# Output tiles of the attention summed in parts between its last heads, decay sums over 128 rows, key rotation spread over four tiles

## The chip, the cores and the metric

One core of a Trainium2 chip runs the kernel alone. The metric is the device time of one execution, in microseconds (us). The engines are TensorE (PE, with its weight loads as PEld), VectorE (DVE), ScalarE (ACT), GpSimd (POOL) and SyncE (SP), which issues the weight transfers. Each engine works through its own list of instructions in order and waits on semaphores for the others.

## The reference, cut to what matters

The input is x, 512 tokens by 1024. Two blocks follow one another: a block of a Mamba-2 layer and an attention layer with latent keys and values, and a block of feed-forward, a second mixer and feed-forward. All matrices are fp32. What the change touches is this:

```python
# Mamba-2 scan, one chunk: decays between tokens from running sums cum of dt * A
seg = cum[:, :, None] - cum[:, None, :]
L = jnp.exp(jnp.where(causal, seg, -jnp.inf))
...
# latent keys and values: the rotated part of the key is shared by all 16 heads
ckv, k_rope = jnp.split(hn @ w_dkv, [KV_LORA], axis=-1)
ckv = rms_norm(ckv, g_ckv)
k_rope = apply_rope(k_rope, cos, sin)
...
# attention of 16 heads, causal; then gate, output projection, residual
cq, gate = jnp.split(h @ w_in, [Q_LORA], axis=-1)
q = (rms_norm(cq, g_q) @ w_uq).reshape(Bsz, S, MLA_HEADS, QK_NOPE + QK_ROPE)
p = jax.nn.softmax(jnp.where(mask, s, -jnp.inf), axis=-1).astype(v.dtype)
o = o.reshape(Bsz, S, MLA_HEADS * V_HEAD) * jax.nn.silu(gate)
return o @ w_out
```

## The kernel before, in words

Activations lie with features on the partitions: a matrix of 1024 features by 512 tokens is eight tiles of 128 x 512. A weight is read in units of at most 128 x 1024 fp32, in the order of `unit_order()`; there are four buffers `raw` for what the transfers bring, and three pairs `wr`/`wl`. Each fp32 value is split into a high part that TensorE's fp32r format holds and the rest. A product is then three matmuls of 128 x 128 by 128 x 512 (`three`, L675 to L678): high by high, high by low, low by high. The high part of a unit is copied by ACT (`hi()`, L1030), the low part is `raw - wr` on DVE (`lo()`, L1324). Both run two units ahead of TensorE (`AHEAD`): a unit's `hi()` waits until the unit three before it is used up (`s_unit`), its `lo()` until `hi()` is done (`s_hi`), and TensorE takes the unit when `s_lo` has counted it. For the eight units `qa`/`qb` of the attention's queries and keys alone, `lo()` makes the high copy on DVE (L1320), ACT does nothing, and POOL makes the low part (L1996). A unit of a 1024-row matrix feeds one output tile: eight steps over its input tiles, 24 matmuls.

The order of work on every engine is written out by hand; there is no planner. `Banks` records in which of the eight PSUM banks a result goes and which semaphore must be reached before the bank may be written again.

The Mamba-2 layer (`first_mixer`). For each pair of heads q = 0 to 15, `decays(q)` (L747) makes two matmuls that spread the row of a head over all partitions: the stationary operand is a column of `pick`, a constant that adds a high and a low row, the moving one is `CH`, 64 rows by 512 (high rows 0 to 31, low rows 32 to 63). ACT turns the result into exponentials `LL` (L1079 to L1088), DVE multiplies them (L1561), and TensorE sums them (L761). Between these stand the tiles of the input projection, one unit each.

The latents (`latents`). Four units `kv_down` give two latent tiles and the key's rotated part in banks 0, 1 and 2. Then eleven output tiles of `mla_in` follow in the order `MLA_ORDER`: four gates, three query latents, four gates. In step i DVE calls `lo()` for the unit two ahead, does side work, and then scales tile i out of PSUM (`SG`, L1659, or the latent, L1651). ACT calls `hi()` and then applies SiLU to the scaled tile (L1169), in this order: so `hi()` of step i+1 stands behind the SiLU of step i, and that behind DVE's scaling of step i. DVE's side work of step 0 is: row scale (L1373), the two latent tiles with their low parts (L1611, L1613), one fold of squares (L1334), and the whole rotation of the key with its copies for the four key buffers `KH` (L1618 to L1634, 12 instructions). The sum of squares `ck` is read on TensorE in step 2 (L686), turned into an inverse root by POOL (L1981 to L1990), and spread in step 4 (L696).

The attention (`attention`). Step h, 0 to 17, does on TensorE: transposes of head h-2 (`turn_most`, L873), scores of head h (L868), the last transposes of head h-2 (`turn_rest`), a projection piece for later heads (`project(h)`, steps 0 to 12 only, L676 to L678 from `CQ` or `CK`), and at odd h the values of a pair (`values`, L896). DVE finds row maxima (L1711) and scales (L1719), ACT makes the exponentials (L1206), scales (L1197) and copies transposed pieces out of PSUM (`PT`, L1182), which frees bank 5 for `turn_rest`. The output of pair j becomes input tile j of the output projection: DVE gates it (`OT`, L1726), ACT makes its high part (L1043), DVE the low part (L1340). After the last step come the eight output tiles `mla_out`, each 24 matmuls; after each tile DVE adds the residual (L1491), ACT squares it twice (L1035, L1039), then makes the next unit's high part. Before TensorE's first projection stands a wait for all eight value tiles in SBUF (`s_vt`, 8). The first pieces use banks 0, 1, 0, of which bank 0 was the last value tile's.

## Time and profile before

| | |
|---|---|
| three timed runs | 1887.38, 1888.96, 1889.33 us; median 1888.96 |
| the profiled execution | 1890.32 us, of which its span is 1888.3 |
| TensorE matmul busy | 1827.4 us, 97% of the span, 8276 matmuls |
| DVE busy | 1035.7 us, 55% |
| ACT busy | 729.0 us, 39% |
| POOL busy | 53.8 us, 3% |
| mean granted clock of TensorE | 0.989 of full |
| transfers | 163.82 MB, queue q1 27.5% of 16 engines |

The span is the time from the first to the last instruction in the profile; the rest of the execution's time lies around it. A row of the timeline gives start and length in us, engine, line, operation, result and inputs, the shape and a count of merged instructions. In brackets stand the engine's idle time before it and what ended it. A matmul's length covers more than its turn, since matmuls overlap: the time that one costs is the distance of two starts. "Granted clock" is TensorE's clock that the throttle let through; 1.00 is 2.4 GHz and 0.5 is 1.2 GHz.

### The profile page before, as it was taken

The numbers are of one execution on the slowest core, as the hardware profiler recorded it, in microseconds if no ns is written. First come the engines' busy times: TensorE is split into PE (matmuls) and PEld (weight loads), VectorE is DVE, ScalarE is ACT, GpSimd is POOL, SyncE is SP. The second block draws the span as 40 slices with busy tenths as digits, with TensorE's granted clock in tenths as the row PEclk, the third lists the DMA queues.
The fourth block names the chain that finished last, engine by engine and source line by source line (L and its number), as shares of the span: only waits on it lengthen the run. The fifth ranks groups of instructions, "written<-read, shape, count | busy, mean of one in ns | idle before, by whom it ended". The sixth has DMA issues, their size and how long they took to land.

```text
span 1888.3 us, 20951 instructions
## 1 busy us (share of the span) xinstructions
PE 1827.4 (97%) x8276; PEld 1460.4 (77%) x8276; DVE 1035.7 (55%) x1484; ACT 729.0 (39%) x1197; POOL 53.8 (3%) x122
## 2 busy tenths in 40 slices
PE   6899999998999899999999999999999999999997
PEld 5677776877866578888888878888888888888886
DVE  6888876666477556444433336555443554444333
ACT  4577776333356643333222243222222333323221
POOL 2000101100120000000000000000000000000000
PEclk9999999999999999999999999999999999999998
DMA  4121212222211023333333422333333333332331
GB/s 149 66 68 67 79 56 78 92 89 70 90 59 34 12 89 91 106 94 100 95 93 94 132 78 80 99 101 92 98 101 100 90 96 94 101 98 90 103 93 53
DMA packets 47041, 163.82 MB, mean 87 GB/s; under 512 B 5216, under 2 KB 5472, under 8 KB 46944
## 3 DMA queue, kind: packets, MB, share of 16 engines
q1 hardware_dynamic: 46656, 162.29, 27.5%
q8 instruction: 66, 1.08, 0.2%
q14 instruction: 31, 0.25, 0.0%
q10 hardware_dynamic: 288, 0.20, 0.0%
HBM read 160.37 MB, written 2.10 MB: 86 GB/s over the span
## 4 chain that ended last, share of the span: by engine, by line
PE 86%; DVE 7%; ACT 4%; issue 2%; POOL 0%; DMA 0%; SPq 0%; DVEq 0%; ACTq 0%; POOLq 0%
PE pb L676 26%; PE pb L678 25%; PE pb L677 25%; PE pb L761 2%; PE pb L868 1%; DVE wl L1324 1%; PE pb L873 1%; PE pb L970 1%; PE pb L972 1%; PE pb L971 1%; DVE XL L1342 1%; ACT wr L1030 1%; PE pb L896 1%; PE pb L686 1%; DVE LL L1561 1%
## 5 line engine op out<-in xcount | busy, mean ns | idle before, releaser
L676 PE MATMUL pb<-XR,wr 128*128 128x512 f32 x1592 | 633.5, 398 | 24.0 <-DVE wl L1324 12.7
L677 PE MATMUL pb<-XL,wr 128*128 128x512 f32 x1592 | 623.5, 392 | 0.0
L678 PE MATMUL pb<-XR,wl 128*128 128x512 f32 x1592 | 623.1, 391 | 0.0
L1324 DVE TENSOR_TENSOR wl<-raw,wr 128x1024 fp32r<-128x1024 f32 (+1 forms) x298 | 359.5, 1206 | 409.9 <-ACT wr L1030 409.0
L1030 ACT ACTIVATE wr<-raw 128x1024 fp32r<-128x1024 f32 (+1 forms) x298 | 309.5, 1038 | 269.3 <-PE pb L678 243.4
L676 PEld LDWEIGHTS pb<-XR,wr 128*128 128x128 f32 x1592 | 301.5, 189 | 97.5 <-issue 27.0
L678 PEld LDWEIGHTS pb<-XR,wl 128*128 128x128 f32 x1592 | 301.0, 189 | 63.8
L677 PEld LDWEIGHTS pb<-XL,wr 128*128 128x128 f32 x1592 | 301.4, 189 | 60.2 <-issue 0.3
L1039 ACT ACTIVATE SQ<-H 128x512 f32<-128x512 f32 x42 | 26.4, 632 | 129.8 <-DVE H L1488 61.2
L676 PE MATMUL pb<-ffn1HR,wr 128*128 128x512 f32 x176 | 68.5, 389 | 0.0
L677 PE MATMUL pb<-ffn1HL,wr 128*128 128x512 f32 x176 | 68.5, 389 | 0.0
L678 PE MATMUL pb<-ffn1HR,wl 128*128 128x512 f32 x176 | 68.5, 389 | 0.0
L676 PE MATMUL pb<-ffn2HR,wr 128*128 128x512 f32 x176 | 68.5, 389 | 0.0
L677 PE MATMUL pb<-ffn2HL,wr 128*128 128x512 f32 x176 | 68.5, 389 | 0.0
L678 PE MATMUL pb<-ffn2HR,wl 128*128 128x512 f32 x176 | 68.5, 389 | 0.0
L1477 DVE SCALAR_TENSOR_TENSOR CV<-U,vec,CV 128x512 f32<-128x512 f32 x72 | 54.3, 754 | 2.6
L676 PE MATMUL pb<-YR,wr 128*128 128x512 f32 x128 | 50.1, 391 | 1.5 <-DVE wl L1324 1.5
L1238 ACT ACTIVATE ffn2HR<-ffn2UP 128x512 fp32r<-128x512 f32 x22 | 13.9, 633 | 97.1 <-DVE ffn2UP L1792 97.1
L678 PE MATMUL pb<-YR,wl 128*128 128x512 f32 x128 | 49.8, 389 | 0.0
L677 PE MATMUL pb<-YL,wr 128*128 128x512 f32 x128 | 49.8, 389 | 0.0
L1238 ACT ACTIVATE ffn1HR<-ffn1UP 128x512 fp32r<-128x512 f32 x22 | 13.9, 633 | 90.4 <-DVE ffn1UP L1792 90.4
L1561 DVE TENSOR_TENSOR LL<-LL,CB 128x1024 f32<-128x1024 f32 (+1 forms) x64 | 48.4, 818 | 0.0
(315 smaller groups left out, 2229.0 us busy)
## 6 DMA issues: line engine op xcount, KB each, us to landing
raw<-in_ffn_in SPq DMA_DIRECT2D x88, 512.0 KB, 3.5
raw<-in_mix_in SPq DMA_DIRECT2D x48, 512.0 KB, 3.5
raw<-in_ssm_in SPq DMA_DIRECT2D x41, 512.0 KB, 3.3
raw<-in_ffn_out SPq DMA_DIRECT2D x32, 512.0 KB, 3.5
raw<-in_ffn_out SPq DMA_DIRECT2D x16, 384.0 KB, 3.1
raw<-in_mla_in SPq DMA_DIRECT2D x11, 512.0 KB, 3.2
raw<-in_ssm_out_a SPq DMA_DIRECT2D x8, 512.0 KB, 3.2
raw<-in_ssm_out_b SPq DMA_DIRECT2D x8, 512.0 KB, 3.3
```

Source lines behind the costliest of these rows:

```text
L676: e.matmul(o, r, xr, start=first, stop=False)
L677: e.matmul(o, r, xl, start=False, stop=False)
L678: return e.matmul(o, l, xr, start=False, stop=last)
L686: m = e.matmul(o[:, at + i:at + i + 1], accs[key][:, 128 * i:128 * i + 128], ones[:, 0:1], start=True, stop=True)
L761: m = e.matmul(y[64 * p:64 * p + 64, 128 * k:S], XD[:, k, j, 64 * p:64 * p + 64], LL[q % 2][:, p, 512 * k:512 * k + S - 128 * k], start=k ...
L868: e.matmul(o[:, at:at + n], q[:, 128 * i:128 * i + 128], kh[:, 0:n], start=True, stop=False)
L1030: e.activation(wr[j % NS][:, 0:width(j)], raw[j % NR][:, 0:width(j)], ACT.Copy).then_inc(s_hi, 1)
L1039: e.activation(SQ[i][:, :], src, ACT.Square, scale=gain).then_inc(s_sq, 1)
L1238: e.activation(HRS[f][:, t, :], UPS[f][t % 2][:, :], ACT.Copy).then_inc(s_hhi, 1)
L1324: e.tensor_tensor(wl[j % NS][:, 0:width(j)], raw[j % NR][:, 0:width(j)], wr[j % NS][:, 0:width(j)].bitcast(F32), ALU.subtract).then_inc(s_ ...
L1477: e.scalar_tensor_tensor(out=cv, in0=u[:, k:k + S], scalar=col("conv_w", 4 * ch + k), in1=cv, op0=ALU.mult, op1=ALU.add).then_inc(then(s_c ...
L1561: m = e.tensor_tensor(x, x, CB[g % 2][:, OFF[k]:OFF[k] + d].unsqueeze(1).to_broadcast([128, 2, d]), ALU.mult)
```

## The change

Five edits:

1. `pick` and `CH` get 128 rows, rows 64 to 127 zero. The 32 matmuls of `decays` are over 128 rows. POOL clears `CH` with one more memset at the start.
2. In the latents, DVE's fold of `ck` and the rotation are spread: fold, first product and two copies in step 1, six instructions in step 2, the last two sums and the three copies to `KH` in step 3. One wait between them is dropped. ACT makes the high copies of the latents ahead of their squares.
3. TensorE's wait for `s_vt` moves from ahead of the projections into `values`. The first three projection pieces use banks 7, 1, 0.
4. `OUT_PARTS`: the matmuls of output tiles 0 and 1, and of tile 2 at the end, are issued step by step between the last heads. A pair (n, t) is three matmuls, tile n over input tile t. 14 pairs stand in steps 13 to 17, ten behind them. The accumulation of tiles 0 and 1 stays open in banks 0 and 1 meanwhile.
5. The high parts of `mla_out` 0 and 1 are made by DVE (in its `lo()` of steps 9 and 10, ahead of the low part), no longer by ACT. High and low part of `mla_out` 2 are made in step 13, no longer after the last head.

```diff
--- before.py
+++ after.py
@@ -105,6 +105,13 @@
     for g in (1, 2, 3):
         out += [[("q", g, 0), ("k", g, 0)], [("q", g, 1)], [("q", g, 2)], [("k", g, 1)]]
     return out + [[], [], []]
+
+OUT_PARTS = {13: [(0, 0), (0, 1)], 14: [(0, 2), (0, 3), (0, 4)], 15: [(0, 5), (1, 0), (1, 1)],
+             16: [(1, 2), (1, 3), (1, 4), (1, 5)], 17: [(0, 6), (1, 6)],
+             18: [(2, 0), (2, 1), (2, 2), (2, 3), (0, 7), (1, 7), (2, 4), (2, 5), (2, 6), (2, 7)]}
 
 
 def ssm_steps():
@@ -321,13 +328,13 @@
-    pick = low("pick", [64, 32], F32R, ph2)
+    pick = low("pick", [128, 32], F32R, ph2)
-    CH = low("CH", [64, S], F32R, ph2)
+    CH = low("CH", [128, S], F32R, ph2)
@@ -440,6 +447,9 @@
 
     seq = unit_order()
     unit = {name: i for i, name in enumerate(seq)}
+
+    POOL_LO = range(unit["qa", 0], unit["qb", 3] + 1)
+    DVE_HI = range(unit["qa", 0], unit["mla_out", 1] + 1)
     steps, last_gates, tail = ssm_steps()
     convs = [x[1] for x in steps if x[0] == "conv"]
     conv_no = {n: i for i, n in enumerate(convs)}
@@ -538,9 +548,13 @@
         for i in range(4):
             bk.place(("v", hf, i), ring.next(), (s_v, 3 * hf + i + 1) if i < 3 else whole("ukv_v", hf),
                      (s_vt, 4 * hf + i + 1))
-    ring = Ring([0, 1])
-
     pieces = head_steps()
+
+    def place_parts(h):
+        for n, t in OUT_PARTS.get(h, ()):
+            if t == 0:
+                bk.place(("mo", n), (0, 1, 2)[n], whole("mla_out", n), (s_res, 8 + n + 1))
+
 
     def place_project(h):
         for kind, g, i in pieces[h + 1]:
@@ -550,8 +564,12 @@
             else:
                 bk.place(("k", g, i), ring.next(), whole(("qa", "qb")[i], g), (s_kh, 4 * g + 2 * i + 2))
 
+    ring = Ring([7, 1, 0])
     place_project(-1)
+    ring = Ring([0, 1])
     for h in range(18):
+        if h == 17:
+            place_parts(h)
         if h >= 2:
             bk.place(("pt", h - 2, 0), 5, (s_turn, 3 * h - 5), (s_pt, 3 * h - 5))
             bk.place(("pt", h - 2, 1), 6, (s_turn, 3 * h - 4), (s_pt, 3 * h - 4))
@@ -563,10 +581,13 @@
             bk.place(("pt", h - 2, 2), 5, (s_turn, 3 * h - 3), (s_pt, 3 * h - 3))
         if h < 16:
             place_project(h)
+        if h < 17:
+            place_parts(h)
         if h >= 3 and h % 2 == 1:
             bk.place(("o", h // 2 - 1), 7, (s_val, h // 2), (s_ot, h // 2))
-    ring = Ring([0, 1, 2, 4, 5, 6])
-    for n in range(8):
+    place_parts(18)
+    ring = Ring([4, 5, 6, 0, 1, 2])
+    for n in range(3, 8):
         bk.place(("mo", n), ring.next(), whole("mla_out", n), (s_res, 8 + n + 1))
 
     def place_ffn(f):
@@ -748,7 +769,7 @@
-                e.matmul(o[:, :], pick[:, h:h + 1].to_broadcast([64, 128]), CH[:, :], start=True,
+                e.matmul(o[:, :], pick[:, h:h + 1].to_broadcast([128, 128]), CH[:, :], start=True,
@@ -888,6 +909,7 @@
         def values(j):
 
             o = opened(("o", j))
+            w.wait_ge(s_vt, 8)
             for k, piece in ((0, 1), (1, 2), (3, 2), (2, 3)):
                 n = S - 128 * k
                 for p in range(2):
@@ -897,11 +919,26 @@
                                  PT[p][:, TOFF[k]:TOFF[k] + n], start=k == 0, stop=k == 2)
             m.then_inc(s_val, 1)
 
+        out_weights = {}
+
+        def out_parts(h):
+            for n, t in OUT_PARTS.get(h, ()):
+                if t == 0:
+                    opened(("mo", n))
+                    out_weights[n] = take("mla_out", n)
+                o, (r, l) = PB[bk.bank["mo", n]], out_weights[n]
+                w.wait_ge(s_xlo, tile_x(3, t))
+                c = slice(128 * t, 128 * t + 128)
+                m = three(o[:, :], r[:, c], l[:, c], XR[:, t, :], XL[:, t, :], t == 0, t == KT - 1)
+                if t == KT - 1:
+                    m.then_inc(s_unit, 1)
+
         def attention():
             w.wait_ge(s_cqlo, 3)
-            w.wait_ge(s_vt, 8)
             project(-1)
             for h in range(18):
+                if h == 17:
+                    out_parts(h)
                 if h >= 2:
                     turn_most(h - 2)
                 if h < 16:
@@ -910,9 +947,12 @@
                     turn_rest(h - 2)
                 if h < 16:
                     project(h)
+                if h < 17:
+                    out_parts(h)
                 if h >= 3 and h % 2 == 1:
                     values(h // 2 - 1)
-            for n in range(8):
+            out_parts(18)
+            for n in range(3, 8):
                 o = opened(("mo", n))
                 r, l = take("mla_out", n)
                 for t in range(KT):
@@ -1021,7 +1061,7 @@ (ACT, hi)
-            if j >= len(seq) or seq[j][0] in ("qa", "qb"):
+            if j >= len(seq) or j in DVE_HI:
@@ -1157,13 +1197,13 @@
                     for t in range(2):
                         w.wait_ge(s_craw, t + 1)
                         w.wait_ge(s_rot, 1)
+                        e.activation(CK[:, 0, t, :], craw[t], ACT.Copy, scale=col("kv_g_latent", t)).then_inc(s_ckhi, 1)
                         square(("ck", t), craw[t])
-                        e.activation(CK[:, 0, t, :], craw[t], ACT.Copy, scale=col("kv_g_latent", t)).then_inc(s_ckhi, 1)
                 if n < 3:
                     w.wait_ge(s_craw, 3 + n)
+                    e.activation(CQ[:, 0, n, :], craw[2 + n], ACT.Copy, scale=col("g_q", n)).then_inc(s_cqhi, 1)
                     w.wait_ge(s_sums, sums_no["ck"])
                     square(("cq", n), craw[2 + n])
-                    e.activation(CQ[:, 0, n, :], craw[2 + n], ACT.Copy, scale=col("g_q", n)).then_inc(s_cqhi, 1)
                 else:
                     w.wait_ge(s_sg, n - 2)
                     e.activation(SG[:, n - 3, :], SG[:, n - 3, :], ACT.Silu).then_inc(s_sgs, 1)
@@ -1205,7 +1245,7 @@
                         n = 128 * (i + 1)
                         e.activation(pp[:, POFF[i]:POFF[i] + n], PB[b][:, at:at + n], ACT.Exp, bias=sm[:, 1, i:i + 1],
                                      scale=SCALE, accum_out=sm[:, 2, i:i + 1]).then_inc(s_exp, 1)
-                if h < 11 and h % 4 in (1, 2):
+                if h < 11 and h % 4 in (1, 2) or h == 13:
                     hi()
                 if h >= 2 and h % 2 == 1:
                     j = h // 2 - 1
@@ -1213,7 +1253,8 @@
                     x_hi(j, OT[:, :], None)
             w.wait_ge(s_gain, 1)
             for n in range(8):
-                hi()
+                if n:
+                    hi()
                 if n == 7:
                     for t in range(7):
                         w.wait_ge(s_mlo, t + 1)
@@ -1313,11 +1354,12 @@
             n_lo[0] += 1
             if j >= len(seq):
                 return
-            if seq[j][0] in ("qa", "qb"):
+            if j in DVE_HI:
                 w.wait_ge(s_hi, j)
                 w.wait_ge(s_raw[j % NR], 16 * (j // NR + 1))
                 w.wait_ge(s_unit, j - NS + 1)
                 e.tensor_copy(wr[j % NS][:, 0:width(j)], raw[j % NR][:, 0:width(j)]).then_inc(s_hi, 1)
+            if j in POOL_LO:
                 return
             w.wait_ge(s_lo, j)
             w.wait_ge(s_hi, j + 1)
@@ -1613,19 +1655,21 @@
                         e.scalar_tensor_tensor(out=CK[:, 1, t, :], in0=craw[t], scalar=col("kv_g_latent", t),
                                                in1=CK[:, 0, t, :].bitcast(F32), op0=ALU.mult,
                                                op1=ALU.subtract).then_inc(s_cklo, 1)
+                if i == 1:
                     fold("ck", 1)
                     w.wait_ge(s_rot, 1)
-                    e.tensor_tensor(TQ[64:128, :], TB[64:128, :], RS[64:128, :], ALU.mult).then_inc(c.up(), 1)
-                    w.wait_ge(c.h, c.n)
+                    e.tensor_tensor(TQ[64:128, :], TB[64:128, :], RS[64:128, :], ALU.mult)
                     e.tensor_copy(TA[64:96, :], TB[96:128, :])
                     e.tensor_copy(TA[96:128, :], TB[64:96, :]).then_inc(c.up(), 1)
+                if i == 2:
                     w.wait_ge(c.h, c.n)
-                    e.tensor_tensor(TS[64:128, :], TA[64:128, :], RS[64:128, :], ALU.mult)
+                    e.tensor_tensor(TS[64:128, :], TA[64:128, :], RS[64:128, :], ALU.mult).then_inc(c.up(), 1)
                     e.tensor_tensor(KH[0][64:96, :], PB[2][64:96, :], TQ[64:96, :], ALU.mult)
-                    e.tensor_tensor(OT[64:96, :], PB[2][96:128, :], TQ[96:128, :], ALU.mult).then_inc(c.up(), 1)
+                    e.tensor_tensor(OT[64:96, :], PB[2][96:128, :], TQ[96:128, :], ALU.mult)
                     w.wait_ge(c.h, c.n)
                     e.tensor_tensor(KH[0][96:128, :], PB[2][64:96, :], TS[64:96, :], ALU.mult)
                     e.tensor_tensor(OT[96:128, :], PB[2][96:128, :], TS[96:128, :], ALU.mult).then_inc(s_kr, 1)
+                if i == 3:
                     w.wait_ge(s_kr, 1)
                     e.tensor_tensor(KH[0][64:96, :], KH[0][64:96, :], OT[64:96, :], ALU.add)
                     e.tensor_tensor(KH[0][96:128, :], KH[0][96:128, :], OT[96:128, :], ALU.subtract).then_inc(c.up(), 1)
@@ -1719,6 +1763,8 @@
                     e.tensor_scalar(p, p, sm[:, 3, 3:4], None, ALU.mult).then_inc(s_pwd, 1)
                 if h < 16:
                     project(h)
+                if h == 13:
+                    lo()
                 if h >= 2 and h % 2 == 1:
                     j = h // 2 - 1
                     w.wait_ge(*bk.full["o", j])
@@ -1729,7 +1775,8 @@
             e.tensor_tensor(gain2[:, :], vec[:, a:a + KT], vec[:, b:b + KT], ALU.mult).then_inc(s_gain, 1)
             w.wait_ge(s_gain, 1)
             for n in range(8):
-                lo()
+                if n:
+                    lo()
                 if n == 7:
                     for t in range(7):
                         x_lo(4, t, H[:, t, :], gain2[:, t:t + 1])
@@ -1932,7 +1979,8 @@
         e.memset(pick[:, :].bitcast(F32), 0.0).then_inc(s_const, 1)
-        w.wait_ge(s_const, 7)
+        e.memset(CH[:, :].bitcast(F32), 0.0).then_inc(s_const, 1)
+        w.wait_ge(s_const, 8)
...
```

## Rows read from the trace of the kernel before

**Rows 1.** Waits of PE: line, who was waited for, us in total, times, longest

```profile
PE pb L676 <- DVE wl L1324: 14.3, 5, 6.0
...
PE pb L873 <- ACT PT L1182: 4.3, 3, 2.0
...
PE pb L873 <- ACT PP L1197: 3.4, 2, 1.7
```

**Rows 2.** Windows: stretch, length, busy time by engine, granted clock, DMA share, GB/s

```profile
84.00:234.00 150.00, 150.00 (x707) 106.52 (x703) 125.89 (x176) 107.70 (x208) 5.21 (x13) 0.99 0.20 67
234.00:294.20 60.20, 57.87 (x278) 41.75 (x277) 40.89 (x58) 45.18 (x90) 0.00 (x0) 1.00 0.18 62
...
594.00:655.20 61.20, 52.13 (x295) 32.76 (x294) 35.79 (x77) 43.17 (x122) 0.00 (x0) 0.97 0.06 18
```

**Rows 3.** Timeline of PE in the latents

```profile
467.04 0.77 PE L676 MATMUL pb<-XR,wr 128*128 128x512 f32 x1 [6.05 <-DVE wl L1324]
...
472.28 0.40 PE L676 MATMUL pb<-XR,wr 128*128 128x512 f32 x1
```

**Rows 4.** Timeline of DVE in the latents

```profile
454.81 0.69 DVE L1334 TENSOR_TENSOR ACC<-ACC,SQ 128x512 f32<-128x512 f32 x1
...
462.13 1.10 DVE L1634 COPY KH<-KH 64x512 f32<-64x512 f32 x3
463.26 0.69 DVE L1659 TENSOR_TENSOR SG<-pb,RS 128x512 f32<-128x512 f32 x1
465.66 1.23 DVE L1324 TENSOR_TENSOR wl<-raw,wr 128x1024 fp32r<-128x1024 f32 x1 [1.71 <-ACT wr L1030]
```

**Rows 5.** Timeline of ACT in the latents

```profile
450.20 0.63 ACT L1035 ACTIVATE ACC<-PP 128x512 f32<-128x512 f32 x1 [5.05 <-DVE PP L1611]
...
463.99 0.63 ACT L1169 ACTIVATE SG<-SG 128x512 f32<-128x512 f32 x1 [9.88 <-DVE SG L1659]
```

**Rows 6.** Timeline of POOL: the root for ck, first and last of 13

```profile
470.59 0.19 POOL L1981 TENSOR_SCALAR RT<-GV 128x4 int32<-128x4 int32 x1 [122.05 <-DVE GV L1380]
...
475.02 0.20 POOL L1990 TENSOR_TENSOR RT<-RT,GW 128x4 f32<-128x4 f32 x1
```

**Rows 7.** Timeline of PE around one pair of decay matmuls

```profile
277.19 0.39 PE L678 MATMUL pb<-XR,wl 128*128 128x512 f32 x1
...
277.87 0.39 PE L678 MATMUL pb<-XR,wl 128*128 128x512 f32 x1
278.19 0.73 PE L751 MATMUL pb<-CH,pick 64*128 64x512 f32 x2
278.85 0.50 PE L676 MATMUL pb<-XR,wr 128*128 128x512 f32 x1
279.18 0.39 PE L677 MATMUL pb<-XL,wr 128*128 128x512 f32 x1
```

**Rows 8.** Timeline of PE at the start of the attention

```profile
526.83 0.47 PE L676 MATMUL pb<-CQ,wr 128*128 128x512 f32 x1 [0.83 <-issue]
...
531.46 0.47 PE L676 MATMUL pb<-CQ,wr 128*128 128x512 f32 x1 [0.94 <-DVE QT L1681]
```

**Rows 9.** Timeline of PE in the last heads, to the first output tile

```profile
609.59 0.44 PE L873 MATMUL pb<-ident,PP 128*128 128x128 f32 x2 [1.98 <-ACT PT L1182]
...
639.47 1.06 PE L873 MATMUL pb<-ident,PP 128*128 128x128 f32 x8 [1.71 <-ACT PP L1197]
...
648.01 0.44 PE L873 MATMUL pb<-ident,PP 128*128 128x128 f32 x2 [1.38 <-ACT PT L1182]
650.16 2.46 PE L873 MATMUL pb<-ident,PP 128*128 128x128 f32 x10 [1.71 <-ACT PP L1197]
...
655.13 0.50 PE L676 MATMUL pb<-XR,wr 128*128 128x512 f32 x1
```

**Rows 10.** Timeline of DVE: low parts of mla_out 0 and 3

```profile
602.98 1.22 DVE L1324 TENSOR_TENSOR wl<-raw,wr 128x1024 fp32r<-128x1024 f32 x1 [3.74 <-ACT wr L1030]
...
663.96 1.23 DVE L1324 TENSOR_TENSOR wl<-raw,wr 128x1024 fp32r<-128x1024 f32 x1 [2.33 <-ACT wr L1030]
```

More of the change, by code:

```diff
@@ L24 @@
 AHEAD = NS - 1
-N_CONST = 16
+N_CONST = 17
 BIG = -3.0e38
@@ L1943, in _ @@
             if i:
-                w.wait_ge(s_const, 10 + i)
+                w.wait_ge(s_const, 11 + i)
             e.affine_select(out=before[:, :], in_=before[:, :], compare_op=ALU.not_equal, fill=1.0, base=-d,
@@ L1950, in _ @@
                         pattern=[[-1, 32]], channel_multiplier=1).then_inc(s_const, 1)
-        w.wait_ge(s_const, 15)
+        w.wait_ge(s_const, 16)
         e.affine_select(out=pick[:, :], in_=pick[:, :].bitcast(F32), compare_op=ALU.not_equal, fill=1.0, base=-32,
@@ L1990, in _ @@
                 e.tensor_tensor(dst[:, :], dst[:, :], GW[:, :], ALU.mult).then_inc(s_groot if i == 2 else c.up(), 1)
-        for j in range(unit["qa", 0], unit["qb", 3] + 1):
+        for j in POOL_LO:
             w.wait_ge(s_lo, j)
```

## The prediction

> **What bounds the kernel now.** I read the page first: TensorE is busy for 97% of the span, so time can only be won where it waits, where its clock is granted at half level, or where one of its instructions takes longer than it must. The view of waits for TensorE comes next [rows 1]: the longest single wait is 6.0 us for a low part made by DVE, and two groups of transposes in the attention wait for ACT, 4.3 and 3.4 us. The windows view [rows 2] then tells stages apart: from 84 to 234 us TensorE never idles, from 234 to 294.2 it loses 60.20 - 57.87 = 2.33 us, and in the last heads, 594 to 655.2, it loses 61.20 - 52.13 = 9.07 us at a mean granted clock of 0.97. Last the timelines at these places [rows 3 to 10]. The normal turn of a 512-column matmul is (277.87 - 277.19) / 3 = 0.227 us, so three take 0.68 and a tile of 24 takes 5.44 [rows 7].
>
> **Decays over 128 rows.** Around a pair of 64-row matmuls, the four starts from 277.87 to 279.18 span 1.31 us where 4 x 0.227 = 0.91 would do: 0.40 us too much, 0.10 at each of the four turns (0.32 or 0.33 for 0.227) [rows 7]. The surplus stands at the turn into the 64-row shape, inside the pair and at two turns behind it, and the streamed columns are the same. So I take it to be the price of another shape, which 128 rows remove. The trace holds no 128-row version; its bounds are 0 and 0.40 us a pair. A loss is excluded: a 128-row matmul of 512 columns has the same 0.39 us row. I take 0.40, since all neighbours of the pair in 128 x 128 shape run at 0.227. There are 16 pairs. Ten fall between 84 and 234 us where TensorE is always busy [rows 2]: nine count whole and the tenth by half, because from its first matmul on ACT and DVE set the pace: 3.8 us. The three between 234 and 294.2 give nothing, they lengthen the 2.33 us wait for a fold that DVE and ACT bring. Of the two ahead of 84 us, half of the first is on the way to the next wait, 0.2. The last counts, 0.4. Sum 4.4, between 0 and 16 x 0.40 = 6.4. POOL's one more memset lies in the first microseconds, while everything waits for the first transfer: nothing.
>
> On this the Trainium skill speaks both ways. "TensorEngine Tiling (Array Packing)", Key Properties, says that a change of the tiling mode drains TensorE; by that the surplus in these rows goes and the sum stands. "TensorE: Matmul & The Clock Gate", Step-by-step, says that a weight load's time goes by its columns and not by its rows; taken alone, that makes 128 rows no cheaper, and the sum would lose its first term. The rows side with the first.
>
> **Rotation spread over four steps.** TensorE idles 6.05 us ahead of the fourth tile, and its first twelve matmuls then take 472.28 - 467.04 = 5.24 us where 12 x 0.227 = 2.72 would do, the half clock that follows the idle time [rows 3]. At stake: 6.05 + 2.52 = 8.6 us. Why it waits: DVE starts the fold at 454.81 and gets to the scaling of tile 0 only at 463.26; 2.40 us behind the scaling (SiLU, high copy on ACT) the low part starts, at 465.66 [rows 4, 5]. Afterwards, in times of this profile: the high copies ahead of the squares save about 0.55 each (a square is 0.63 long [rows 5]), so the scaling of tile 0 starts at 454.81 - 1.1 = 453.7. The moved block is 8.45 us: 1.13 for the three copies, and 11 others by 0.665. Steps 1, 2 and 3 get 4, 5 and 2 of these plus the copies: 2.66, 3.33, 2.46. A step is then 1.13 (low part) + side work + 2.40, and the low parts of tiles 3, 4, 5, 6 start at 456.1, 462.3, 469.3 and 475.3 (0.1 for `ck` counted in) and take 1.23 us. TensorE, which ended tile 2 at 460.99, asks for them at 461.0, 466.4, 471.9 and 477.7: slack 3.7, 2.9, 1.4, 1.2. Nothing waits, but two steps have little to spare. What is late next is the spread of `ck`: its sum is now read behind the step-2 work, at 466.8; POOL's 13 instructions take 475.22 - 470.59 = 4.63 us [rows 6], so the root is there at 471.6 and TensorE asks at 466.4 + 7 x 0.68 = 471.2. Some 0.4 us remain. Gain 8.1, bounds 6.0 (the clock stays low once) and 8.6.
>
> **Start of the attention.** The first piece waits 0.83 us for the last value tile to leave bank 0, the third 0.94 us for the first piece's bank [rows 8]; with banks 7, 1, 0 and `s_vt` later both are gone. The fourth piece now gets bank 0 straight behind the third and waits about 0.5 for DVE, whose work begins a microsecond earlier. With 0.1 for each weight load no longer bare, 1.5 us; bounds 0.6 and 1.9.
>
> **Output parts between the heads.** Moved: 14 pairs of 0.68 = 9.5 us of matmuls. As work they cost before what they cost after, so the gain is idle time filled and clock kept: 9.07 us, of which 1.98, 1.71, 1.38 and 1.71 are the large waits [rows 2, 9]; and the granted clock of 0.97 is 2 x 0.03 x 61.2 = 3.7 us at half level, of which I count 1.3 as lost on running matmuls (the last values and transposes, 650.16 to 655.13). At stake 10.4. The 1.98 goes by another edit: in step 9 DVE stood 3.74 us for ACT's high copy [rows 10], and now makes it itself in less than the 1.22 of its low part; the OT of that step, ACT's XR and behind it the PT that bank 5 waits for come 2.5 us earlier. From there ACT and DVE run ahead of TensorE until step 13. Walking the queues on, I find left over: 0.4 ahead of the transposes in step 13, 0.5 in step 14 (DVE's new `lo()` of `mla_out` 2 delays that pair's OT; queued behind it are OT, XR and PT), 0.3 in step 15, 1.0 in step 16 where parts stand behind `turn_rest` and not ahead of it, 0.4 in step 17: 2.6. Each return from fp32 transposes or scores to the split matmuls costs 0.1, seven times: 0.7. A new wait comes behind the last head: the high part of tile 3 sits on ACT behind tile 0's squares. Before, tile 0 was complete (5.44 + 0.3 behind 655.13, at 660.9) and the low part of tile 3 at 663.96 + 1.23 = 665.2 [rows 9, 10], 4.3 later; now only five pairs, 3.4 us, cover that: 0.9. Net 10.4 - 2.6 - 0.7 - 0.9 = 6.2, bounds 2 and 9.5. The first term to fail here would be the walk.
>
> **Sum.** 4.4 + 8.1 + 1.5 + 6.2 = 20.2 us. The profiled execution took 1890.32 us (span 1888.3), which gives 1870.1; the median of the runs is 1.4 lower than it, so 1868.8.
>
> **The rivals.**
> A: the shape is not what costs, the stationary operand read as a repeated column is. The pairs keep their 0.40: 1873.2. For it: nothing else in the trace loads weights so. Against it: the turns behind the pair, with ordinary weights, are long too [rows 7].
> B: in the last heads the loop of maxima, exponentials and scales on DVE and ACT sets the pace, and parts ahead of `values` push it back. Then only the waits of 1.98 and about 0.7 fall: gain 2 instead of 6.2, 1873.0. For it: 1.71 us waits for a scale by ACT [rows 9]. Against it: in this stretch ACT is busy 43.17 and DVE 35.79 of 61.2 us [rows 2].
> C: the slack of 1.2 us in the latents is not there; tiles 5 and 6 and the spread wait 1 to 1.5 us each and the clock falls once more. Gain 4: 1872.9.
> D, slower: the clock. Place: the last heads and the eight output tiles. Here many short waits stand among small matmuls, and after the waits of 1.38 and 1.71 the clock did fall. If the parts, being broken up by transposes, no longer lift it and it stays at the lower level through the output tiles, each of their 192 matmuls costs 0.20 more (5.24 / 12 less 0.227 [rows 3]): 38 us, 1868.8 + 38 = 1907. It decides from 100 such matmuls on. Against it: from 84 to 234 us, with transposes in between, the clock is 0.99 [rows 2].
>
> **How the numbers follow.** The forecast gets 0.62, with 1865.5 to 1872 as its own range; A 0.13, B 0.12, C 0.06, D 0.03; 0.04 is for A with B, 1877. The bounds of all terms together reach from 26.4 us (1862.6) to 8.6 us (1880.4). Leaving out D, the pair and the far end of the bounds, the range is 1863 to 1876. About 0.2% (3.8 us) is what a measurement of this kernel tells from no change. Every case but D is beyond that on the fast side: faster 0.95, same 0.02, slower 0.03.
>
> **What would show it.** Right: the 6.05 us wait and the half clock behind it are gone; L751 shows 128 x 512 and four turns of 0.23; the first projection starts straight behind the last value tile; TensorE's idle time from the tenth head to the first whole output tile is under 4 us, with one wait of about 0.9 for a low part ahead of tile 3. Wrong: turns of 0.33 around L751 (A); waits of over 1 us for ACT in steps 14 to 17 (B); waits for low parts in steps 3 to 6 of the latents (C); a granted clock of 0.5 in the output tiles (D). The forecast is wrong as a whole if less than 13 us are won.

## The result: 20.9 us faster

The changed kernel took 1868.24 us (median of 4 runs, 1867.85 to 1869.61) against 1889.14 (4 runs, 1887.38 to 1890.06). The ratio is 0.9893, with a 95% interval of 0.9881 to 0.9904. The forecast was 1868.8. The profiled execution took 1867.85 us, its span is 1866.1.

The page of the changed kernel, its first lines (lines of code have moved: L676 to L678 are now L697 to L699, L1324 is L1366, L873 is L894):

```profile
span 1866.1 us, 20948 instructions
...
PE 1816.2 (97%) x8276; PEld 1459.5 (78%) x8276; DVE 1036.0 (56%) x1486; ACT 727.7 (39%) x1195; POOL 57.2 (3%) x123
```

TensorE's instructions are the same in number; its busy time fell by 11.2 us, its idle time by 11.0. The waits of TensorE, against [rows 1]:

```profile
PE pb L697 <- DVE XL L1384: 10.6, 4, 7.8
PE pb L697 <- DVE wl L1366: 9.2, 4, 5.4
PE pb L707 <- DVE TB L1376: 3.7, 1, 3.7
...
PE pb L894 <- ACT PT L1222: 1.6, 3, 0.9
PE pb L717 <- POOL RT L2038: 1.5, 1, 1.5
```

The 6.0 us for a low part is gone (the 5.4 is an old one in the first 50 us), the waits for PT fell from 4.3 to 1.6, the waits for PP, the tile of exponentials, are gone. Three sizes are new: 3.7 us for the fold of TB, a tile in which DVE adds up squares, which was 2.4; 1.5 for POOL's root; and 10.6 in all for low parts XL of input tiles, which was 9.5. Of this last growth 0.87 us stands ahead of the first matmul of the feed-forward, where the timelines have a wait of 0.70 us before and 1.57 now. The windows of [rows 2], for the changed kernel:

```profile
84.00:234.00 150.00, 150.00 (x727) 112.29 (x724) 127.51 (x179) 111.13 (x220) 5.19 (x13) 1.00 0.22 71
234.00:294.20 60.20, 56.49 (x271) 41.92 (x270) 42.89 (x59) 41.90 (x79) 0.00 (x0) 0.97 0.18 62
...
594.00:655.20 61.20, 58.09 (x311) 39.91 (x310) 32.14 (x65) 38.01 (x100) 0.00 (x0) 1.00 0.10 31
```

The changed kernel is ahead of the old one by 1.9 us at the first of these windows and by more at each later one, so they don't hold quite the same work. In the same 150 us TensorE runs 727 matmuls and not 707. The 0.97 of the second window is the half clock behind the wait for TB (288.70), which before lay outside of it (294.25). From 594 to 655.2 TensorE idles 3.1 us (61.20 - 58.09) instead of 9.07, at full clock, but this window now starts about 16 us further into the work; a comparison of equal work follows below.

The timeline of TensorE in the last heads and ahead of output tile 3 of the changed kernel, for [rows 9]; these are all its waits of over 0.2 us between 608 and 677 us:

```profile
619.50 0.44 PE L894 MATMUL pb<-ident,PP 128*128 128x128 f32 x2 [0.47 <-ACT PT L1222]
...
632.17 0.44 PE L894 MATMUL pb<-ident,PP 128*128 128x128 f32 x2 [0.92 <-ACT PT L1222]
...
637.87 0.44 PE L894 MATMUL pb<-ident,PP 128*128 128x128 f32 x2 [0.25 <-ACT PT L1222]
...
648.82 0.47 PE L697 MATMUL pb<-XR,wr 128*128 128x512 f32 x1 [1.16 <-DVE wl L1366]
```

Below, "the late stretch" is the time from the transposes of step 9 to the first matmul of the feed-forward: 594.45 to 699.69 in the kernel before, 105.24 us, and 578.90 to 677.84 in the changed one, 98.94. By the windows view TensorE is idle in it for 9.46 us before and 4.68 now, and busy for 95.78 and 94.26, at a mean granted clock of 0.98 and 1.00. How far one profile can be trusted here: in three runs below that leave this stretch as it was before it took 105.29, 105.72 and 106.57 us, and in three that leave it as changed 98.89, 98.89 and 98.91. The clock makes the difference: busy time goes among the first three from 95.85 to 97.31.

### The profile page after: what moved, and what is told of

It is laid out like the page before. It is cut to its first block, busy times and chain, and to the rows that moved or that the text cites. A ratio compares the mean times of both kernels' runs of the same rounds, so it can differ in the third digit from the quotient of the medians.

```text
span 1866.1 us, 20948 instructions
## 1 busy us (share of the span) xinstructions
PE 1816.2 (97%) x8276; PEld 1459.5 (78%) x8276; DVE 1036.0 (56%) x1486; ACT 727.7 (39%) x1195; POOL 57.2 (3%) x123
## 4 chain that ended last, share of the span: by engine, by line
PE 86%; DVE 7%; ACT 4%; issue 2%; POOL 1%; DMA 0%; DVEq 0%; ACTq 0%; POOLq 0%
PE pb L697 25%; PE pb L698 25%; PE pb L699 25%; PE pb L782 2%; PE pb L889 1%; DVE wl L1366 1%; ACT wr L1070 1%; PE pb L894 1%; PE pb L918 1%; PE pb L1010 1%; PE pb L1012 1%; PE pb L1011 1%; DVE XL L1384 1%; PE pb L707 1%; DVE LL L1603 1%
## 5 line engine op out<-in xcount | busy, mean ns | idle before, releaser
L697 PE MATMUL pb<-XR,wr 128*128 128x512 f32 x1592 | 631.1, 396 | 20.2 <-DVE XL L1384 10.6
L699 PE MATMUL pb<-XR,wl 128*128 128x512 f32 x1592 | 622.4, 391 | 0.0
L1366 DVE TENSOR_TENSOR wl<-raw,wr 128x1024 fp32r<-128x1024 f32 (+1 forms) x298 | 359.7, 1207 | 403.1 <-ACT wr L1070 402.3
L697 PEld LDWEIGHTS pb<-XR,wr 128*128 128x128 f32 x1592 | 300.8, 189 | 88.5 <-issue 17.3
L699 PEld LDWEIGHTS pb<-XR,wl 128*128 128x128 f32 x1592 | 300.4, 189 | 63.5
L697 PE MATMUL pb<-ffn1HR,wr 128*128 128x512 f32 x176 | 68.5, 389 | 0.0
L699 PE MATMUL pb<-ffn1HR,wl 128*128 128x512 f32 x176 | 68.5, 389 | 0.0
L697 PE MATMUL pb<-ffn2HR,wr 128*128 128x512 f32 x176 | 68.5, 389 | 0.0
L699 PE MATMUL pb<-ffn2HR,wl 128*128 128x512 f32 x176 | 68.5, 389 | 0.0
L697 PE MATMUL pb<-YR,wr 128*128 128x512 f32 x128 | 50.1, 391 | 1.6 <-DVE wl L1366 1.6
L699 PE MATMUL pb<-YR,wl 128*128 128x512 f32 x128 | 49.8, 389 | 0.0
```

What stands on the lines that cost most here:

```text
L697: e.matmul(o, r, xr, start=first, stop=False)
L699: return e.matmul(o, l, xr, start=False, stop=last)
L1366: e.tensor_tensor(wl[j % NS][:, 0:width(j)], raw[j % NR][:, 0:width(j)], wr[j % NS][:, 0:width(j)].bitcast(F32), ALU.subtract).then_inc(s_ ...
```

## Each edit alone, on the kernel before

All four ran on one chip against one series of the kernel before (median 1888.34).

**e1_decay.** Edit 1 alone.

```diff
-    pick = low("pick", [64, 32], F32R, ph2)
+    pick = low("pick", [128, 32], F32R, ph2)
-    CH = low("CH", [64, S], F32R, ph2)
+    CH = low("CH", [128, S], F32R, ph2)
```

> The kernel before with edit 1 alone: 128 rows in pick and CH, the column of pick still repeated. If the other shape is what costs, the turns at the decay matmuls fall from 0.33 to 0.23 us, TensorE reaches the wait for the fold of TB (294.25 us before) 3.8 to 4.0 us earlier counted from the end of the wait ahead of the first scan sums (83.12), that wait grows by about 1.2, and the kernel is 4.4 us faster (0.2%). Rival A, the repeated column costs: turns of 0.33, no gain.

Measured: 1883.68 us, ratio 0.9978 (0.9969 to 0.9987), 4.7 us. Around the pair that answers to [rows 7], in the timeline of TensorE of this run:

```profile
272.88 0.39 PE L678 MATMUL pb<-XR,wl 128*128 128x512 f32 x1
273.10 0.63 PE L751 MATMUL pb<-CH,pick 128*128 128x512 f32 x2
273.57 0.39 PE L676 MATMUL pb<-XR,wr 128*128 128x512 f32 x1
273.80 0.40 PE L677 MATMUL pb<-XL,wr 128*128 128x512 f32 x1
```

Four starts from 272.88 to 273.80 span 0.92 us, which is 4 x 0.23; before it was 1.31. The column of `pick` is still a repeated one, so rival A falls. The loads show what went: in the kernel before the load of the 64-row pair starts at 278.19, together with its matmul, here at 272.88, while the matmul ahead of it runs. From the first scan sums to the fold of TB it takes 290.18 - 82.71 = 207.47 us where the kernel before took 294.25 - 83.12 = 211.13: 3.66 us, and the wait there grew from 2.38 to 3.70.

**e2_rotation.** Edit 2 alone (the diff ahead of the prediction, DVE's `latents` and ACT's order of copy and square).

> The kernel before with edit 2 alone: rotation spread over steps 1 to 3, high copies ahead of squares. Forecast theory: the 6.05 us wait for a low part and the half clock behind it go, 8.1 us faster, and what remains is a wait for POOL's root of ck. The whole change shows that wait at 1.55 us and not at 0.4, so 7.0 us is now expected. Rival C, the four steps have no slack: waits for low parts of 1 us and more in steps 3 to 6 and a gain of 4.

Measured: 1881.71 us, ratio 0.9964 (0.9951 to 0.9978), 6.6 us. From the last wait ahead of the latents to the first projection piece it takes 520.55 - 447.78 = 72.77 us, before 526.83 - 447.09 = 79.74: 6.97 us, as expected. There is one wait in between, 1.53 us for POOL's root; no tile waits for a low part.

**e3_parts.** Edits 4 and 5 alone.

> The kernel before with edits 4 and 5 alone: output parts between the last heads, high parts of mla_out 0 and 1 on DVE, mla_out 2 prepared in step 13. Forecast theory: 6.2 us faster, waits of 0.5 and 0.9 for PT and one of 0.9 to 1.2 for the low part of tile 3. Rival B, ACT and DVE set the pace there: 2 us faster, waits of over 1 us for ACT in steps 14 to 17.

Measured: 1881.18 us, ratio 0.9967 (0.9955 to 0.9980), 7.2 us. The late stretch is 692.63 - 593.72 = 98.91 us, 6.33 less than the kernel before. Waits of 0.45, 0.92 and 0.25 for PT and 1.16 for tile 3; none of over 1 us for ACT, so rival B's sign is absent.

**e4_banks.** Edit 3 alone.

```diff
-            w.wait_ge(s_vt, 8)
             project(-1)
...
+    ring = Ring([7, 1, 0])
     place_project(-1)
+    ring = Ring([0, 1])
```

> The kernel before with edit 3 alone: banks 7, 1, 0 for the first three pieces and the wait for the value tiles moved into the values. Forecast theory: 1.5 us faster, the waits of 0.83 and 0.94 us become one of about 0.5 us for the evacuation of the third piece. Rival: DVE, which evacuates the pieces, sets the pace up to the first scores, and the gain is under 0.5 us.

Measured: 1885.46 us, ratio 0.9990 (0.9981 to 0.9999). That is 2.9 us by the medians, with an interval that almost reaches none. By the profile, the way from the latents' wait to the transposes of step 5 is 562.00 - 465.05 = 96.95 us, before 565.44 - 467.04 = 98.40: 1.45 us. One wait of 0.57 stands for the two of [rows 8].

The four medians are 4.7 + 6.6 + 7.2 + 2.9 = 21.4 us below the kernel before; all edits together gave 20.9. Each of these has an interval of 2 to 3 us to either side, so the stretches say it better: 3.66 us for the decays alone and 3.61 in the changed kernel (288.70 - 81.18 = 207.52 where it was 211.13); 6.97 + 1.45 = 8.42 for the rotation and the start of the attention and 8.50 together (549.86 - 440.01 = 109.85 where it was 565.44 - 447.09 = 118.35); 6.33 and 6.30 for the last heads. The edits do not get in each other's way.

## The changed kernel with one thing altered

**e5_act_high.**

```diff
-    DVE_HI = range(unit["qa", 0], unit["mla_out", 1] + 1)
+    DVE_HI = range(unit["qa", 0], unit["qb", 3] + 1)
```

> The changed kernel with the high parts of mla_out 0 and 1 made by ACT again, as before. Forecast theory: these copies on ACT, and DVE's wait for them, cause the 1.98 us wait for PT in step 10 and most of the smaller ones in steps 11 to 13 (0.36, 0.96, 0.66), which the parts of steps 13 to 17 cannot fill: they return, 2 to 4 us slower than the whole change. Rival: the parts alone do the work and the whole is less than 1 us slower.

Measured: 1873.34 us, ratio 0.9923 (0.9910 to 0.9937) against 0.9893 for the whole change. The late stretch is 682.09 - 578.78 = 103.31 us, 4.4 longer; 2 to 4 were expected, and the rival, under 1, falls. The timeline of TensorE shows the wait back, with half clock behind it (0.69 us where 0.44 stood in [rows 9]), and a second one; those of 0.36 and 0.96 did not return. From 594 to 598 the mean granted clock is 0.58. Of the 4.4 us 2.3 are idle time and 2.0 busy time:

```profile
593.92 0.69 PE L894 MATMUL pb<-ident,PP 128*128 128x128 f32 x2 [1.97 <-ACT PT L1222]
...
612.21 1.09 PE L894 MATMUL pb<-ident,PP 128*128 128x128 f32 x8 [0.66 <-DVE PP L1763]
```

**e7_parts_last.**

```diff
-OUT_PARTS = {13: [(0, 0), (0, 1)], ..., 18: [(2, 0), ...]}
+OUT_PARTS = {18: [(n, t) for n in range(3) for t in range(8)]}
```

> The changed kernel with all 24 pairs of output tiles 0 to 2 behind the last head, tile after tile; high parts as in the change. Forecast theory: waits of 1.7, 1.4 and 1.7 us for ACT in steps 15 to 17 come back, those of steps 10 to 13 stay away, the wait of 1.16 for tile 3 goes: about 2.6 us slower than the whole change. Rival B, ACT and DVE set the pace in the last heads: no slower than the whole change.

Measured: 1875.76 us, ratio 0.9935 (0.9923 to 0.9948). The late stretch is 685.79 - 578.64 = 107.15 us: 8.2 longer than with the parts between the heads, not 2.6, and longer than before the change; rival B's "no slower" falls. The wait of 1.16 us for tile 3 is gone, as expected. The timeline of TensorE has a pair of waits that the forecast had not named, and half clock behind them:

```profile
619.22 0.44 PE L892 MATMUL pb<-ident,PP 128*128 128x128 f32 x2 [1.84 <-ACT PT L1220]
...
621.71 1.97 PE L892 MATMUL pb<-ident,PP 128*128 128x128 f32 x8 [2.05 <-DVE PP L1761]
...
633.08 0.44 PE L892 MATMUL pb<-ident,PP 128*128 128x128 f32 x2 [1.37 <-ACT PT L1220]
...
635.23 2.46 PE L892 MATMUL pb<-ident,PP 128*128 128x128 f32 x10 [1.71 <-ACT PP L1235]
```

Most of the 8.2 us is clock: over the late stretch TensorE is busy for 99.53 us at a mean granted clock of 0.94, where the changed kernel has 94.26 at 1.00. That is 5.3 us; only 2.9 are idle time.

**e11_high_only.** As the last, and `mla_out` 2 prepared behind the last head as in the kernel before.

```diff
-                if h < 11 and h % 4 in (1, 2) or h == 13:
+                if h < 11 and h % 4 in (1, 2):
...
-                if h == 13:
-                    lo()
```

> The changed kernel with all 24 pairs behind the last head and mla_out 2 prepared there too, so that of edits 4 and 5 only the high parts of mla_out 0 and 1 on DVE are left. If it was the copies of mla_out 2 in step 13 that made the waits of 1.84 and 2.05 us in the run with the parts last, they go here, and the waits that stay are the 1.4 and two of 1.7 of the kernel before: 4 us faster than that run in the last heads. If the two waits stay, the cause is elsewhere.

Measured: 1870.47 us, ratio 0.9903 (0.9886 to 0.9919). The late stretch is 680.78 - 579.91 = 100.87 us, 6.3 shorter than in e7 where 4 was expected; 4.2 of that is busy time (95.28 for 99.53), the clock again. The two waits of 1.84 and 2.05 are gone, so the copies of `mla_out` 2 in step 13 made them. The timeline of TensorE keeps exactly the three late waits of [rows 9]:

```profile
620.58 1.06 PE L892 MATMUL pb<-ident,PP 128*128 128x128 f32 x8 [1.71 <-ACT PP L1235]
...
629.12 0.44 PE L892 MATMUL pb<-ident,PP 128*128 128x128 f32 x2 [1.38 <-ACT PT L1220]
631.27 2.00 PE L892 MATMUL pb<-ident,PP 128*128 128x128 f32 x10 [1.71 <-ACT PP L1235]
```

So of the 6.3 us that edits 4 and 5 win, 105.24 - 100.87 = 4.4 come from the high copies of two weight units that changed engine. The parts with their preparation in step 13 bring 100.87 - 98.94 = 1.9 more. e5 gives the same in the other order: parts without the moved copies win 105.24 - 103.31 = 1.9, and the copies then 4.4. These are differences of single profiles, and the stretch before varied by 1.3 us. The preparation in step 13 alone, with nothing to fill the wait it makes, costs 6.3.

**e10_square_first.** ACT's squares of the latents ahead of the high copies again.

> The changed kernel with ACT making the squares of the latents ahead of their high copies again, as before; rotation spread as in the change. By the forecast's sums the low parts of tiles 3 to 6 come 1.1 us later against slacks of 3.7, 2.9, 1.4 and 1.2, so TensorE waits for none of them; the root of ck comes 1.1 us later, so that wait grows from 1.55 to about 2.6: 1.1 us slower than the whole change. Rival C, no slack: waits for low parts besides, 2 us and more slower.

Measured: 1870.25 us, ratio 0.9905 (0.9891 to 0.9920). In the latents TensorE waits once, by its timeline:

```profile
468.69 0.62 PE L717 MATMUL pb<-ident,RT 128*128 128x128 f32 x4 [2.58 <-POOL RT L2038]
```

1.03 us more than 1.55, and no tile waits for its low part though all came later. The slack was there; rival C falls. The medians say 2.0 us, within their intervals.

**e6_ck_first.**

```diff
                 if i == 2:
+                    sum_of("ck", 256)
                     w.wait_ge(c.h, c.n)
...
-                if i == 2:
-                    sum_of("ck", 256)
```

> The changed kernel with the sum of ck read by DVE ahead of the five rotation products of step 2 and not behind them, 3.6 us earlier. If the 1.55 us wait for the root stands only on when POOL starts and how long it takes, it goes, and the kernel is 1.5 us faster than the whole change. In the changed kernel POOL's chain took 5.5 us and not 4.6, with four operations of 0.4 to 1.1 in place of 0.20 while DVE ran operations with both inputs in SBUF. If such DVE operations hold POOL up, single POOL operations are long here too, but only beside those, and 0.2 beside those that read PSUM; if not, they are long at other places.

Measured: 1866.88 us, ratio 0.9886 (0.9872 to 0.9899). The wait is gone. The medians' gain over the whole change, 1.4 us, is within the intervals; the profile shows it. From 440.01 to the wait at 520.50 the changed kernel needs 80.49 us, this one 519.68 - 440.90 = 78.78, 1.7 less where 1.5 was expected. POOL's chain, the 13 operations of [rows 6], took 461.25 - 457.21 = 4.0 us. Its first operation is the only long one, the other twelve take 0.19 to 0.20. The first two, beside DVE's, in the timelines of both engines:

```profile
457.15 0.69 DVE L1667 TENSOR_TENSOR TS<-TA,RS 64x512 f32<-64x512 f32 x1
457.21 0.69 POOL L2028 TENSOR_SCALAR RT<-GV 128x4 int32<-128x4 int32 x1 [113.65 <-DVE GV L1422]
457.87 0.69 DVE L1668 TENSOR_TENSOR KH<-pb,TQ 32x512 f32<-32x512 f32 x1
457.98 0.20 POOL L2032 TENSOR_TENSOR GW<-RT 128x4 f32<-128x4 f32 x1
```

**e8_both_waits and e9_all.** What the waits of 1.16, 0.92 and 0.47 us pointed to; e9 adds e6's edit.

```diff
-                if n:
+                if n != 1:
                     hi()
...
-             16: [(1, 2), (1, 3), (1, 4), (1, 5)], ...
+             "16a": [(1, 2)], 16: [(1, 3), (1, 4), (1, 5)], ...
...
+                out_parts(f"{h}a")
                 if h >= 2:
                     turn_rest(h - 2)
```

(The first hunk is in ACT's list alone. Step 14 is split likewise, with (0, 2) ahead.)

> The changed kernel with two edits more: ACT makes the high part of mla_out 3 ahead of the squares of tile 0, and in steps 14 and 16 one part each stands ahead of turn_rest. Expected: the wait of 1.16 us ahead of tile 3 goes, those of 0.47 and 0.92 for PT shrink by up to 0.7 each: 2.0 us faster than the whole change. Rival: the squares, now later, delay the folds and the next low parts, and the wait comes back ahead of tile 4.

Measured: 1865.42 us, ratio 0.9880 (0.9867 to 0.9894). The late stretch is 674.81 - 578.51 = 96.30 us, 2.6 less than 98.94, and no output tile waits behind the last head, so the rival falls; the wait ahead of the feed-forward is 1.05 us and not 1.57. A wait of 0.58 for PP came up in step 15, those for PT fell to nothing, 0.22 and 0.25.

> The changed kernel with all three additions: ck's sum read first in step 2, the high part of mla_out 3 ahead of the squares, one part each ahead of turn_rest in steps 14 and 16. If the waits are separate, the gains add: 1.5 for ck and 3.0 for the other two as the last run's profile has them, together 3.5 to 4.5 us faster than the whole change, about 1864.

Measured: 1862.70 us, ratio 0.9865 (0.9850 to 0.9880), which lies below the interval of the whole change. It is the fastest version here, 5.5 us below the changed kernel by the medians of different series, where 3.5 to 4.5 were expected. Part of that is luck with the clock: in its profile alone no half clock follows the first scan sums, and from these to the fold of TB it takes 287.12 - 81.28 = 205.84 us, where all other profiles with edit 1 have 207.4 to 207.6. Its four runs lie in two pairs, 1861.5 and 1861.7, 1863.7 and 1863.9.

## Why the prediction was right, step by step

**Decays.** Shape, not repetition: shown by e1. Nine and a half pairs were to give 3.8 us between 83 and 294; 3.66 came. The three pairs behind only lengthened the wait, from 2.38 to 3.70. The two small terms: 0.2 us ahead of 83 came (36.18 us from 46 to the first scan sums in e4, which lacks edit 1, and 36.01 in e1; the kernel before had 37.02, but this stretch varies by 0.8 between profiles of like kernels). The last pair was put at 0.4, and e1 gained 1.12 between the fold of TB and the next wait (96.14 us from 290.18 to 386.32, 97.26 from 294.25 to 391.51). This pair stands at half clock in both, and its four turns took 2.30 us before (296.48 to 298.78) and 1.71 in e1 (292.88 to 294.59).

The loads of the pair kept their length (185 ns before, 187 now); what went was that they stood bare. The Trainium skill has a rule that changing the tiling mode drains TensorE, in "TensorEngine Tiling (Array Packing)", Key Properties; these rows agree with it. The Trainium skill's other rule, that a weight load's time goes by columns, in "TensorE: Matmul & The Clock Gate", Step-by-step, agrees with the two lengths, but was no ground to expect nothing.

**Rotation.** The wait for the low part and the half clock behind it went, as forecast. The term was too large: 6.97 us and not 8.1, because of the root of `ck`, which TensorE waits 1.55 us for and not 0.4. Its start was forecast at 466.8 in times of the old profile, which is 459.7 in the new one, and DVE wrote the sum at 459.77. But POOL's chain took 5.5 us instead of 4.63 [rows 6]. (466.8 and 4.63 make 471.4; the prediction has 471.6.) The timelines of POOL and DVE in the changed kernel show where:

```profile
462.38 1.23 DVE L1366 TENSOR_TENSOR wl<-raw,wr 128x1024 fp32r<-128x1024 f32 x1 [1.72 <-ACT wr L1070]
462.55 1.11 POOL L2033 TENSOR_TENSOR GW<-RT 128x4 f32<-128x4 f32 x1
463.63 0.68 DVE L1674 TENSOR_TENSOR KH<-KH,OT 32x512 f32<-32x512 f32 x1
463.74 0.64 POOL L2006 TENSOR_TENSOR GW<-GW,GV 128x4 f32<-128x4 f32 x1
464.33 0.69 DVE L1675 TENSOR_TENSOR KH<-KH,OT 32x512 f32<-32x512 f32 x1
464.46 0.61 POOL L2036 TENSOR_SCALAR GW<-GW 128x4 f32<-128x4 f32 x1
465.05 1.10 DVE L1678 COPY KH<-KH 64x512 f32<-64x512 f32 x3
465.16 0.38 POOL L2038 TENSOR_TENSOR RT<-RT,GW 128x4 f32<-128x4 f32 x1
```

An operation of POOL over 128 x 4 elements, else 0.20 us, ends with the operation of DVE beside it (463.66 with 463.61, 464.38 with 464.31, 465.07 with 465.02). The forecast moved such DVE operations beside the chain and took its old length. That length already held one stretched operation, which stands between the two that [rows 6] show. In the timelines of POOL and DVE of the kernel before:

```profile
472.81 1.23 DVE L1324 TENSOR_TENSOR wl<-raw,wr 128x1024 fp32r<-128x1024 f32 x1 [1.71 <-ACT wr L1030]
472.83 1.26 POOL L1990 TENSOR_TENSOR RT<-RT,GW 128x4 f32<-128x4 f32 x1
```

**Start of the attention.** 1.45 us against 1.5, and the wait of 0.57 against 0.5. The first piece starts straight behind the last value tile (511.56 and 511.79 in the changed kernel).

**Last heads.** 6.3 us against 6.2, but the number hides two errors. The first is in the walk. It had 0.4, 0.5, 0.3, 1.0 and 0.4 of waits left in steps 13 to 17 and 0.9 ahead of tile 3, 3.5 in all; 0.47 (step 14), 0.92 (step 16), 0.25 (step 17) and 1.16 (tile 3) are there, 2.8. It put nothing on the wait ahead of the feed-forward, and that grew by 0.87, to 3.7 in all. Behind the last head DVE and ACT start late with tile 3 and then take 4.84 us a tile (low parts at 656.45, 661.28, 666.12, 670.96) against TensorE's 5.44; at the last tile they have not caught up.

The second is what each edit is worth. Where the prediction prices rival B, it gives 2 us to the moved high copies (the waits of 1.98 and about 0.7), which leaves 4.2 for the parts. Measured, it is the other way round: the copies are worth 4.4 (e11 against the kernel before, e5 against the changed one) and the parts with their preparation 1.9. That the total came out is luck. The parts are worth 8.2 (e7) only against a kernel in which step 13 prepares `mla_out` 2 with nothing to cover it: ACT's 1.04 and DVE's 1.23 us there then go into TensorE's waits, and half clock behind these makes 5.3 of the 8.2, which is rival D's mechanism in the small. In the changed kernel the stage ran at 1.00, so D did not come. B did not come either, as no wait of over 1 us for ACT is left in steps 14 to 17; but the parts brought less than the forecast gave them.

**The whole.** Of the 22.2 us between the two spans 2.1 are not the change's: 0.9 stands ahead of the first decay (46.10 and 45.17 for the same matmul), 0.8 between there and 83, which e4 has too without any edit to that stretch, and 0.35 behind the start of the feed-forward. The other 20.1 are 5.3 for the decays (0.2, 3.6 and 1.5 behind the fold of TB) where 4.4 was forecast, 8.5 for rotation and start where 9.6 was, and 6.3 where 6.2 was. So the forecast of 20.2 was also right because a term that was 1.1 too large met one that was 0.9 too small.

Half clock lies at other places in the first 90 us from run to run. Behind the wait for TB it lasted 6.8 us before and 3.4 after. This is no accident of one profile: all eight profiles of the changed kernel and its variants have 3.4, and 95.67 to 95.73 us from the fold of TB to the next wait; the kernel before, e2, e3 and e4 have 6.8 and 97.24 to 97.29, and e1, with the same wait of 3.7 us as the changed kernel, 6.8 and 96.14. Why edit 1 alone does not shorten it stays open.

## What to carry to other kernels

An edit that only moves work between engines' queues can be worth more than the one it accompanies: 4.4 us here against 1.9. Price each half without the other. When a block is spread over steps, put whatever another engine is waiting for ahead of it, as e6 did. Filler matmuls between dependent stages pay most where the wait they fill would be followed by half clock, as in e7.

## What the runs showed of the hardware that was not expected

POOL's operation does not end until DVE's does when DVE reads two operands from SBUF. The rows of e6 and of the changed kernel show it: 1.11, 0.64 and 0.61 us beside `raw - wr` and two sums of `KH`, 0.69 beside `TA` by `RS`, but 0.20 beside products that read one operand from PSUM. The kernel before has it once, 1.26 beside `raw - wr`. The Trainium skill has this as a rule in "SBUF — State Buffer", section "SBUF: two separate sides": DVE with two SBUF inputs and GpSimd reading SBUF take turns for a whole instruction. These traces agree: each of these operations ends within 0.06 us of DVE's. By it, and by the 1.26 us in the trace of the kernel before, the longer chain was there to be seen before. The 0.38 us beside the copies of `KH`, which e2 and e10 have too, suggest that a DVE operation with one operand can do the same for a shorter time; no run tries that alone.

Two 64-row matmuls amid 128-row ones cost 0.39 us more than two of 128 rows with half of them zero (1.31 and 0.92 us for four turns).
